# Four late modulation steps moved from the GLA levels into the first input projection, on one core of a Trainium2 chip

## What is computed

```
mod = silu(cond) @ mod_w[i] + mod_b[i]          # cond: c and c_ctx, 2 rows; i = 0, 1
x1  = rms_norm(x) * norm_mix * (1 + scale) + shift
z   = x1 @ ev_w_in                               # 512 rows, 2336 columns: the first input projection
...                                              # gated linear attention (GLA) both ways, full attention
```

## Time and profile before

| | |
|---|---|
| median of 3 runs | 2045.27 us (2043.88 to 2045.29) |
| profiled execution | 2042.26 us, of it 2040.5 us span |
| mean granted TensorE clock | 0.929 |
| PE busy | 1742.2 us (85%) |
| DVE busy | 1156.1 us (57%) |
| ACT busy | 970.5 us (48%) |
| DMA over the span | 335.84 MB, mean 165 GB/s |

### The profile page before, as it was taken

How to read it: one execution, slowest core, us unless ns; L and a number is a source line. 1 busy time by engine, 2 the same in 40 slices (tenths; PEclk the granted TensorE clock), 3 DMA queues, 4 the chain that set the end, 5 groups by cost and what they waited for, 6 DMA issues and landing times.

```text
span 2040.5 us, 24999 instructions
## 1 busy us (share of the span) xinstructions
PE 1742.2 (85%) x9822; PEld 1379.4 (68%) x9822; DVE 1156.1 (57%) x1857; ACT 970.5 (48%) x1683; POOL 101.1 (5%) x135
## 2 busy tenths in 40 slices
PE   5996878994699973898899998988889969989987
PEld 2783447773577763666799997866678637757866
DVE  2217674446588865764566667435753484464454
ACT  5213223625588865464344443535555534544563
POOL 0000100001100002100000002000000000000000
PEclk7998888997899996999899998998999989999998
DMA  7224996011999982202255554432035303514521
GB/s 304 83 101 167 348 339 247 1 44 59 367 423 421 421 325 95 102 1 83 94 188 188 188 185 144 172 117 83 1 113 187 143 1 134 188 60 147 193 83 42
DMA packets 52691, 335.84 MB, mean 165 GB/s; under 512 B 5488, under 2 KB 5488, under 8 KB 18288
## 3 DMA queue, kind: packets, MB, share of 16 engines
q1 hardware_dynamic: 46112, 310.04, 40.6%
q0 software_dynamic: 6480, 24.44, 3.1%
HBM read 305.10 MB, written 29.36 MB: 164 GB/s over the span
## 4 chain that ended last, share of the span: by engine, by line
PE 66%; DVE 13%; ACT 10%; DMA 6%; issue 3%; POOL 1%; SPq 0%; POOLq 0%; DVEq 0%; ACTq 0%
PE bank L1235 17%; PE bank L1237 17%; PE bank L1236 17%; DMA ring_float<-weights_dram 4%; ACT hT_float L730 2%; DVE ring_float32r L2074 2%; ACT arena_float L784 2%; PE bank L1269 1%; PE bank L1432 1%; ACT ring_high L683 1%; PE bank L1558 1%; PE bank L1606 1%; PE bank L1550 1%; DVE stat L2741 1%; PE bank L1395 1%
## 5 line engine op out<-in xcount | busy, mean ns | idle before, releaser
L2074 DVE TENSOR_TENSOR ring_float32r<-ring_float,ring_high 128x1024 fp32r<-128x1024 f32 x298 | 355.3, 1230 | 369.3 <-ACT ring_high L683 369.1
L683 ACT ACTIVATE ring_high<-ring_float 128x1024 fp32r<-128x1024 f32 x298 | 301.4, 1059 | 412.9 <-DMA ring_float<-weights_dram 410.4
L1235 PE MATMUL bank<-ring_high,x_float32r 128*128 128x512 f32 x608 | 243.4, 400 | 5.6 <-DVE mix_float32r L2103 3.0
L1237 PE MATMUL bank<-ring_high,mix_float32r 128*128 128x512 f32 x608 | 241.2, 397 | 0.0
L1236 PE MATMUL bank<-ring_float32r,x_float32r 128*128 128x512 f32 x608 | 241.1, 397 | 0.0
L1235 PE MATMUL bank<-ring_high,arena_float32r 128*128 128x512 f32 (+1 forms) x368 | 139.6, 379 | 17.3 <-DVE arena_float32r L2103 6.6
L1235 PE MATMUL bank<-Z_float32r,ring_high 128*128 128x256 f32 x512 | 146.0, 285 | 8.0 <-issue 4.2
L1236 PE MATMUL bank<-Z_float32r,ring_high 128*128 128x256 f32 x512 | 146.1, 285 | 0.0
L1237 PE MATMUL bank<-Z_float32r,ring_float32r 128*128 128x256 f32 x512 | 145.9, 285 | 0.0
L1235 PEld LDWEIGHTS bank<-ring_high,x_float32r 128*128 128x128 f32 x608 | 116.0, 191 | 34.6 <-ACT hT_float L730 5.7
L1237 PE MATMUL bank<-ring_high,arena_float32r 128*128 128x512 f32 (+1 forms) x368 | 137.9, 375 | 0.0
(11 more groups left out here) (405 smaller groups left out, 3330.2 us busy)
## 6 DMA issues: line engine op xcount, KB each, us to landing
ring_float<-weights_dram SPq DMA_DIRECT2D x234, 1024.0 KB, 4.8
Z_float<-weights_dram SPq DMA_DIRECT2D x33, 1024.0 KB, 8.7
sent<-post_row SPq DMA_DIRECT2D x1, 11776.0 KB, 38.1
Z_float<-sent SPq DMA_DIRECT2D x23, 512.0 KB, 9.1
made<-mix_float POOLq DMA_DIRECT2D x23, 512.0 KB, 7.9
post_row<-norm_post_dram POOLq DMA_DIRECT2D x4, 512.0 KB, 4.4
small<-small_dram SPq DMA_DIRECT2D x1, 1072.0 KB, 9.2
x_float<-x_dram SPq DMA_DIRECT2D x1, 1024.0 KB, 5.3
```

The costliest lines, as they stand in the source:

```text
L683: nc.scalar.activation(ring_high[:, slot, half], ring[:, slot, half], ACT.Copy).then_inc(high_ready, 1)
L1235: nc.tensor.matmul(out, left[0], right[0], start=start, stop=False)
L1237: return nc.tensor.matmul(out, left[1], right[0], start=False, stop=stop)
L2074: ve.tensor_tensor(ring_low[:, slot, half], ring[:, slot, half], ring_high[:, slot, half], ALU.subtract).then_inc(low_ready, 1)
```

## The change

Four of the late steps are taken out of GLA and done in the first input projection. A step is cut into its halves (`mod_half`): the first half, with the turn of the step before, stands behind the first chunk of each of the four blocks of 512 columns, the second half behind the second chunk. The chunks in HBM are put in that order (`IN0_AT` gives the places of the projection's chunks). On ACT, the copy of the step stands behind the last bank copy of the block, and the split of chunk 2n+3 no longer stands ahead of the block's bank copies: they go first. In the levels a step now follows each direction's two pair sets (`s == 1`), so two per level, and `MOD_LEVEL` on ACT is 2. The masks' load stays ahead of the first chunk of `mod_late`, which is now eight chunks later.

```diff
-MOD_GATES, MOD_START, MOD_LEVEL = 1, 2, 3
+MOD_BETWEEN = 4
+MOD_GATES, MOD_START, MOD_LEVEL = 1, 2, 2
...
+IN0_AT = [STREAM["in0"][0] + 2 * c for c in range(9)]
...
-    w += chunks_of(np.concatenate([ev[:, 0:1536], ev[:, 1568:2336]], 1))
-    w += mod[2 * MOD_EARLY:]
+    in0 = chunks_of(np.concatenate([ev[:, 0:1536], ev[:, 1568:2336]], 1))
+    for c in range(2 * MOD_BETWEEN):
+        w += [in0[c], mod[2 * MOD_EARLY + c]]
+    w += [in0[8]] + mod[2 * MOD_EARLY + 2 * MOD_BETWEEN:]
...
+                at = (lambda c: first + c) if first != STREAM["in0"][0] else (lambda c: IN0_AT[c])
...
-                    if first is not None and w == 512 and start + SLOTS == made < n_chunks:
+                    if first is not None and first != STREAM["in0"][0] and w == 512 and start + SLOTS == made < n_chunks:
-                        chunk_high(first + made)
+                        chunk_high(at(made))
...
-                    projected(columns(zs[0], NT, [512, 512, 512, 512, 256]), STREAM["in0"][0])
+                    projected(columns(zs[0], NT, [512, 512, 512, 512, 256]), STREAM["in0"][0],
+                              after=lambda n, t: mod_copy(mod_rows_late, int(t == NT - 1 and n < MOD_BETWEEN)))
...
-            def mod_step(rows):
-                for kh in range(2):
-                    w = chunk().rearrange("p (k n) -> p k n", k=4)
...
+            def mod_half(rows, kh):
+                w = chunk().rearrange("p (k n) -> p k n", k=4)
+                if kh == 0 and mod_steps[0] not in (0, MOD_EARLY):
+                    mod_turn(rows)
+                for k in range(4):
+                    i = nc.tensor.matmul(mod_bank[32 * k:32 * k + 2, :], cond[:, 4 * kh + k, :], w[:, k, :],
+                                         start=(kh == 0), stop=(kh == 1), tile_position=(0, 32 * k))
...
+            def mod_step(rows):
+                for kh in range(2):
+                    mod_half(rows, kh)
...
+                        if after_chunk:
+                            after_chunk(n, k0 // rows_per)
...
-                            if (d, s) != (0, 0):
+                            if s == 1:
                                 mod_late(1)
...
-                    project("first", NT, [(NT, 512)] * 4 + [(NT, 256)])
+                    project("first", NT, [(NT, 512)] * 4 + [(NT, 256)],
+                            after_chunk=lambda n, kh: mod_half(mod_rows_late, kh) if n < MOD_BETWEEN else None)
```

More of the change, by code:

```diff
@@ L121 @@
 STREAM, N_LOADS = fields(
-    [("mod_early", 2 * MOD_EARLY), ("in0", 9), ("mod_late", 2 * (MOD_STEPS - MOD_EARLY)), ("out0", 4),
+    [("mod_early", 2 * MOD_EARLY), ("in0", 9 + 2 * MOD_BETWEEN), ("mod_late", 2 * (MOD_STEPS - MOD_EARLY - MOD_BETWEEN)), ("out0", 4),
      ("experts0", len(RING_CHUNKS)),
@@ L1260, in mod_turn @@
                 return i
-            def mod_step(rows):
-                for kh in range(2):
-                    w = chunk().rearrange("p (k n) -> p k n", k=4)
-                    if kh == 0 and mod_steps[0] not in (0, MOD_EARLY):
-                        mod_turn(rows)
-                    for k in range(4):
-                        i = nc.tensor.matmul(mod_bank[32 * k:32 * k + 2, :], cond[:, 4 * kh + k, :], w[:, k, :],
-                                             start=(kh == 0), stop=(kh == 1), tile_position=(0, 32 * k))
-                    if kh == 0:
-                        chunk_done(i)
+            def mod_half(rows, kh):
[5 more added lines that the diff above has]
+                                         start=(kh == 0), stop=(kh == 1), tile_position=(0, 32 * k))
+                if kh == 0:
+                    chunk_done(i)
+                    return
                 mod_steps[0] += 1
@@ L1298, in transposes, with project @@
                     i.then_inc(a_full, 1)
-            def project(name, T, blocks, between=None):
+            def project(name, T, blocks, between=None, after_chunk=None):
                 hT = split_views(name, T)
@@ L2673, in first_layer @@
                 features_low("first", NT)
-                chunks_low(first + 1, SLOTS - 1)
+                for c in range(1, SLOTS):
+                    chunk_low(IN0_AT[c] if i == 0 else first + c)
                 if i == 0:
-                    chunks_low(first + SLOTS, 9 - SLOTS)
+                    for c in range(SLOTS, 9):
+                        chunk_low(IN0_AT[c])
                     gla()
```

3 lines of the change are left out of this document (2 added, 1 removed).

## The result

| | before | changed |
|---|---|---|
| median of the timed runs | 2044.58 us (2038.61 to 2045.29) | 2017.65 us (2014.35 to 2018.18) |
| ratio, 95% interval | | 0.9873 (0.9856 to 0.9890) |
| profiled execution | 2042.26 us | 2014.35 us |

What follows compares the result with a forecast made beforehand. PE was taken to bound the projection, and chunk loads with PE's steps the levels, where DVE waited. Levels gain 24.0 less 7.8 projection and 0.5 gate products gave 15.7 us: 2029.6 us predicted, 8-in-10 range 2021 to 2040.

Steps and rivals of the forecast that it cites:

- Cost in the projection: First input projection: PE time added by four moved steps (halves, turns, return to split products), 7.8 us, all on the path.
- late copies: Projection, ACT: a slow chunk landing delays a block's bank copies by 0.8 us; 0 taken, 3.2 us in the range.
- the rule of drains: Projection, PE: changing tiling mode drains TensorE; sixteen seams at 0.16 us would add 2.6 us; not taken, the row preferred.
- The gain in the levels: GLA levels: time saved by two steps a level instead of mostly three; 24.3 us reckoned, 24 taken.
- Left-over 2.5 + 3.4 = 5.9: Levels: DVE waits expected to remain, 2.5 us at full clock plus 3.4 for PE at half clock.
- the upper bound (a): Levels: gain if DVE never waits, 105.8 - 75.6 = 30.2 us.
- (b): Levels: gain if PE sets the pace, 13.3 us for four steps plus 3.8 of chunk waits, 17.1 us.
- (c): Levels: gain if loads set the pace, eight fewer chunks at 3.1 us each, 24.9 us.
- DVE never waits: Rival 3, levels: DVE waits vanish, gain 30.2 us, time 2023.4; chance 0.10.
- PE at half clock in the levels (1): Rival, levels: PE stays at 1.2 GHz, gain about nothing against cost 8.3 us, time 2053.6; chance 0.06.
- Waits for chunks (2): Rival, levels: PE's waits for chunks stay whole, only its time goes, 13.3 us, time 2040.3; chance 0.10.
- Late splits (4): Rival, projection: seven chunks land 3 us later than there is room for, 21 us added, time 2050.6; chance 0.04.

Runs made afterwards that it cites:

- the repeat: Both kernels run again unchanged, for a second profile each: before 2045.69 us, changed 2020.77 us, ratio 0.9887.
- two_old_places: Changed kernel, still two steps a level, but at two old places, one between the second direction's two pair sets: 2030.24 us, ratio 0.9936.
- levels_bare: Changed kernel with all steps left for the levels put behind the first pair products, none in the levels: 2092.06 us, ratio 1.0237.
- before_late1: Kernel before, plus one useless ACT copy in the second layer, ahead of its last normalisation: 2045.25 us, ratio 1.0001.
- six_at_start: Kernel before, nothing moved to the projection; six steps instead of two ahead of the levels, two per level at the change's places: 2033.30 us, ratio 0.9945.

## Why the prediction was right in sign and wrong in size

- **What bounds the two stretches** was right. PE sets the projection, at its full cost; the levels were set by steps and their chunks, and "late next is DVE" came true.
- **Cost in the projection**: 7.8 us forecast, 7.6 and 7.7 measured. First halves 0.97 each as said, turns 0.88 for 0.98, second halves in the hole 0.01 for 0.1, and going back to the split products 0.11 behind each first half and 0.03 behind each second, 0.6 us as said. The rest of the 7.6 is 0.10 ahead of the first half and a start of the projection at 1.2 GHz that was longer in this profile; over all profiles the cost is 7.0. The splits were never late. The range's 3.2 us for late copies did not come, and the rule of drains did not add its 2.6 us. That rule (the Trainium skill, TensorEngine Tiling (Array Packing), Key Properties: a change of tiling mode drains TensorE) gives no price. The trace agrees that a change costs something, 0.32 us for both seams of the first half, but the terms taken from rows held nearly all of it (0.11 in the 0.97, 0.11 in the going back), so the row decided rightly. Nothing here shows that it is a drain: a product behind a mere pause also took 0.31 us to the next.
- **Gate products**: 0.5 forecast, 0.4 measured.
- **The gain in the levels, 24.0, was mis-sized; this is the first step that failed.** The term was "Left-over 2.5 + 3.4 = 5.9" against the upper bound (a) of 30.2. Measured: 2.1 us of DVE waits (2.9 in the repeat) and a gain of 28.8 (31.1). The 3.4 was priced from half clock as it stood in the old levels, where PE waited for chunks. The bounds were also reckoned for too few steps. "Four gone" and "eight fewer" chunks hold for the kernel, but the stretch lost four and a half steps, nine chunks: by the prediction's own rates (b) is 19.2 in place of 17.1 and (c) 28.0 in place of 24.9, and 24 was taken for being near (c). And the earlier trace rows left out the first level, 14.93 us with three steps, where little was to be had. In the new levels four of six lines have a clock of 1.00; the one at 0.65 took 14.48 us for 14.31 of DVE. Only the first, at 0.79, lost 1.6. That 28.8 is near the corrected (c) does not make the loads the pace: two_old_places loads 25 chunks in 89.89 us, against 24 in 76.99, and levels_bare takes 74.50 with none. The rival "DVE never waits" (2023.4, given 0.10) was nearly the case, and I gave it too little: 3.1 us a chunk was no floor, since one of the new levels loads at 374 GB/s, 2.8 us a chunk.
- **The tail, the second step that failed**: "nothing takes the gain back that I can find" held the tail constant and had no term for it either way. It was 7.8 us shorter in this pair (4.3 in the repeat). Against the forecast for the profiled execution, 2026.6, the time was 2014.35: 4.8 us from the levels, 7.8 from the tail, 0.3 from the costs, less 1.0 for a later start, leave 0.3 us. With the levels sized right the forecast for the median would have been 2024.8 and the range would have held it; what is left to 2017.65 goes with the shorter tail, which in the traces goes with the clock behind the levels. Why the change should have it stays open, and by how much the lower end, 2021, was missed is in part chance: 3.4 us here, 0.2 in the repeat (2020.77).
- **Rivals.** PE at half clock in the levels (1) did not come: even where the clock was low, it did not set the pace. Waits for chunks (2) did not stay whole: 16.0 to 6.1 us in all. Late splits (4) did not come: no wait of PE for a split of a weight chunk is in the trace. That the place of the steps, not only their number, carries the gain was in my working (a wait of 0.35 us between sets) but in no rival; the prediction read it as two steps a level, and two_old_places shows that this alone would have given half of the result.

**What to carry to other kernels.** Filler work that drags its own transfers along belongs where those transfers find DMA idle and the engine that does it is kept busy: there it costs its bare work, 1.9 us a step in the projection, against 4.8 us at the start of the levels. Inside a stretch bound by a consumer it belongs behind a group of sets that the consumer has cover for, not between two sets it takes at once: the place was worth nearly as much as the count. The floor of such a stretch is the consumer's busy time, and a version without any filler reads it off in one run. Count the pieces that leave the stretch you price, not the pieces that the edit moves. And later stretches can fall differently between the clock's two levels, several us here in either direction, from one kernel to the next and from one execution to the next; no sum contains it, so the range has to.

## What the runs showed of the hardware

- Nearly the same instructions behind the levels took 1728.5 to 1737.7 us, with 199 to 240 us of it at 1.2 GHz. That is up to 0.5%, more than most single terms of this case. One and the same piece took 58.84 and 58.97 us at a mean clock of 0.83, and 55.97 at 0.88. Repeated runs of one kernel spread by 8 to 10 us to either side (2035.41 to 2052.94 around 2045.25 in before_late1).
- A first half of four products in four column tiles, in a stream of 128x128 products, costs 0.97 us from start to start, 0.86 of it its four products, and the product behind it is another 0.11 late; a second half in the hole of 0.89 us costs 0.01, and 0.03 behind it.
- Low clock on PE is harmless where it isn't the pace: 0.65 in one level of the change, and 0.72 over the levels in levels_bare, both within 0.7 us of DVE's busy time. The same low clock is dear where steps stand alone on the path: in six_at_start, at 0.56, four more steps took 19.2 us.
